# Modulation rows in one go ahead of the indexer's scores, logits inside the recurrence's last pass, and matmul moving operands at the weights' remainder by 256 bytes

## What is computed

```python
mod = jnp.dot(silu(c), w_ada) + b_ada            # 6 x 1024 values
sh1, sc1, ga1, sh2, sc2, ga2 = split(mod, 6)
xn = rms_norm(h, g_mix) * (1.0 + sc1) + sh1
q, k, v, qi, ki, wi, xr, yr, gate_a, gate_b = split(xn @ w_in + b_in)
attn = dsa_attention(q, k, v, qi, ki, wi, rel_bias)   # 8 indexer heads score, top 128 keys
rnn = rg_lru(causal_dwconv(xr), ...) * gelu(yr)
h = h + ga1 * ((sigmoid(gate_a) * (attn @ w_o_attn) + sigmoid(gate_b) * (rnn @ w_o_rnn)) @ w_out)
xn = rms_norm(h, g_ffn) * (1.0 + sc2) + sh2
h = h + ga2 * ((silu(conv(gate)) * conv(val)) @ w_down)
# second block: [meta; h] -> w_in_2 (9 x 1024 columns) -> HGRN2 and convolution -> w_out_2,
# then w_up_2, w_down_2, final norm, meta tokens dropped
```

## Time and profile before

| | |
|---|---|
| runs | 1821.69 us median of 3, 1819.59 to 1823.01 |
| profiled execution, own time | 1822.29 us |
| its span | 1820.4 us |
| mean granted TensorE clock | 0.985 of 2.4 GHz |
| busy: PE, PE weight loads, POOL, DVE, ACT | 97%, 86%, 81%, 59%, 29% |
| matmuls | 11430, each with a weight load |

### The profile page before, as it was taken

One profiled execution on the slowest core, in us unless ns is written; L12 is line 12 of the kernel. 1 busy time (PEld: TensorE's weight loads), 2 busy tenths in 40 slices (PEclk: granted clock), 3 DMA queues, 4 the chain that ended last, 5 costly groups with the idle time before them and its releaser, 6 DMA issues.

```text
span 1820.4 us, 33550 instructions
## 1 busy us (share of the span) xinstructions
PE 1766.3 (97%) x11430; PEld 1565.1 (86%) x11430; DVE 1068.6 (59%) x1677; ACT 526.4 (29%) x775; POOL 1476.2 (81%) x2245
## 2 busy tenths in 40 slices
PE   4889999999999999999899999999999999999997
PEld 2667776677899999888799999999999999999886
DVE  6887987845566777522656655665665455555102
ACT  3235664330221111100443443443343211111001
POOL 1869996559899999999678877876886999989885
PEclk8899999999999999999999999999999999999999
DMA  9644232222222222333222222222221322222332
GB/s 365 237 155 137 87 100 83 103 94 93 91 90 90 90 91 91 101 103 98 67 71 81 82 70 71 82 70 70 82 82 59 102 94 92 92 92 92 104 104 93
DMA packets 55328, 184.42 MB, mean 101 GB/s; under 512 B 6673, under 2 KB 9905, under 8 KB 55250
## 3 DMA queue, kind: packets, MB, share of 16 engines
q1 hardware_dynamic: 52018, 177.53, 29.7%
q10 hardware_dynamic: 3232, 5.77, 0.9%
HBM read 178.56 MB, written 4.72 MB: 101 GB/s over the span
## 4 chain that ended last, share of the span: by engine, by line
PE 91%; DVE 3%; POOL 2%; DMA 2%; ACT 1%; issue 1%; SPq 1%; ACTq 0%; DVEq 0%; POOLq 0%
PE gp L400 28%; PE gp L401 28%; PE gp L402 27%; PE A L727 2%; POOL Wlo L391 1%; DMA AW<-ada 1%; PE A L526 1%; DMA raw<-units 1%; PE A L496 1%; PE A L559 1%; PE gp L585 1%; PE A L774 0%; PE A L577 0%; PE A L723 0%; SPq L328 0%
## 5 line engine op out<-in xcount | busy, mean ns | idle before, releaser
L391 POOL TENSOR_TENSOR Wlo<-raw,Whi 128x256 fp32r<-128x256 f32 x1120 | 974.9, 891 | 46.8
L400 PE MATMUL gp<-XNhi,Whi 128*128 128x264 f32 (+3 forms) x2736 | 848.6, 310 | 26.9 <-POOL Wlo L391 18.3
L401 PE MATMUL gp<-XNlo,Whi 128*128 128x264 f32 (+3 forms) x2736 | 837.0, 306 | 0.0
L402 PE MATMUL gp<-XNhi,Wlo 128*128 128x264 f32 (+3 forms) x2736 | 834.2, 305 | 0.0
L400 PEld LDWEIGHTS gp<-XNhi,Whi 128*128 128x128 f32 x2736 | 517.9, 189 | 65.9 <-POOL Wlo L391 19.8
L401 PEld LDWEIGHTS gp<-XNlo,Whi 128*128 128x128 f32 x2736 | 518.1, 189 | 24.4 <-issue 2.2
L402 PEld LDWEIGHTS gp<-XNhi,Wlo 128*128 128x128 f32 x2736 | 517.1, 189 | 23.4
L387 POOL TENSOR_TENSOR probe<-raw 1x1 f32<-1x1 f32 x560 | 181.1, 323 | 278.3 <-PE gp L402 211.5
L388 POOL TENSOR_SCALAR Whi<-raw 128x512 fp32r<-128x512 f32 x560 | 346.0, 618 | 0.0
L400 PE MATMUL gp<-AChi,Whi 128*128 128x512 f32 (+1 forms) x374 | 142.8, 382 | 0.0
L402 PE MATMUL gp<-AChi,Wlo 128*128 128x512 f32 (+1 forms) x374 | 142.6, 381 | 0.0
(11 more groups left out here) (314 smaller groups left out, 2270.5 us busy)
## 6 DMA issues: line engine op xcount, KB each, us to landing
raw<-units SPq DMA_DIRECT2D x280, 512.0 KB, 3.5
AW<-ada SPq DMA_DIRECT2D x40, 512.0 KB, 7.1
AWL<-ada SPq DMA_DIRECT2D x8, 512.0 KB, 3.6
bias_rows<-RB ACTq DMA_DIRECT2D x1, 2560.0 KB, 20.9
H<-xT SPq DMA_DIRECT2D x1, 2048.0 KB, 8.3
BIAS<-bias_rows ACTq DMA_DIRECT2D x1, 2048.0 KB, 8.9
out<-H SPq DMA_DIRECT2D x8, 256.0 KB, 2.2
WG<-gatew ACTq DMA_DIRECT2D x8, 128.0 KB, 2.0
```

Source lines behind the costliest of these rows:

```text
L391: ins = pool.tensor_tensor(lo[:, c:c + UNIT // 4], src[:, c:c + UNIT // 4], hi[:, c:c + UNIT // 4].bitcast(F32), ALU.subtract)
L400: pe.matmul(dst, Whi[s][:, k, :], rhi, start=start, stop=False)
L401: pe.matmul(dst, Whi[s][:, k, :], rlo, start=False, stop=False)
L402: return pe.matmul(dst, Wlo[s][:, k, :], rhi, start=False, stop=stop)
```

## The change

It has three parts, and one smaller one for the wait at the norm.

**Addresses and spans.** `XNhi`, `XNlo`, `M2hi` and `M2lo` get rows of 576 words (2304 bytes, nine times 256). A tile `fill` of 56 words moves what lies behind it. Norms write `XN` at `x0` = 0 for both 512-word and 514-word uses in the first block, at 2 or 0 in the second block's, and at 16 only for the mixer, where the 528-word product starts at 0. Spans become 256 + 272 and 256 + 258. The built program then has `Whi0` at 63104, `XNhi` at 18048, `XNlo` at 36480, `AChi` at 117888, `MGhi` at 183424, `RNhi` at 134272, `M2hi` at 117888, `M2lo` at 136320, all with remainder 128. So d is 0 for every product of units, but for the second half of each pair in the second `up`, which starts 2 words on (d = 8).

**DVE's order.** All 24 rows in one go ahead of the scores, the small chain behind the scores and ahead of block 0's convolution, and `logits(0, 0, 1)` between the last scan and its product.

**Norm.** Nine plain fp32 matmuls of 256 words into an unused part of `gp1` after `stats(2)`; the wait for `con_in` moves ahead of them.

```diff
+ROW = 576
-AHEAD = [0, 4, 2, 2, 3, 3, 3, 3, 2, 2]
+AHEAD = [0, 4, 4, 4, 3, 4, 3, 2]
 def spans(n):
-    return [(0, n)] if n <= 512 else [(0, (n // 2 + 1) // 2 * 2), ...]
+    return [(0, n)] if n <= 512 else [(0, HALF), (HALF, n - HALF)]
...
-        XNhi = sb("XNhi", [P, KC, T], F32R)
-        XNlo = sb("XNlo", [P, KC, T], F32R)
+        XNhi = sb("XNhi", [P, KC, ROW], F32R)
+        XNlo = sb("XNlo", [P, KC, ROW], F32R)
...
+        sb("fill", [P, 56])
...
-            M2hi = sb("M2hi", [P, KC, T], F32R, f)
+            M2hi = sb("M2hi", [P, KC, ROW], F32R, f)
...
-        NORMS = [dict(c0=META, n=S, feeds=0, h0=None), dict(c0=META, n=S, feeds=1, h0=0),
-                 dict(c0=META, n=S, feeds=2, h0=KC), dict(c0=META - 2, n=S + 2, feeds=3, h0=2 * KC),
+        NORMS = [dict(c0=META, x0=0, n=S, feeds=0, h0=None), dict(c0=META, x0=2, n=S, feeds=1, h0=0),
+                 dict(c0=META, x0=META, n=S, feeds=2, h0=KC), dict(c0=META - 2, x0=0, n=S + 2, feeds=3, h0=2 * KC),
...
                     load_mid(ADA_FIRST + c)
-            sp.dma_start(CON[:, C_ONE:], consts[:, C_ONE:]).then_inc(con_in, 16)
+                if u == len(AHEAD) - 1:
+                    sp.dma_start(CON[:, C_ONE:], consts[:, C_ONE:]).then_inc(con_in, 16)
...
             stats(2)
-
+            pe.wait_ge(con_in, 16)
+            for _ in range(9):
+                pe.matmul(gp[1][:, 1024 - HALF:1024], ident, CON[:, 0:HALF], start=True, stop=True)
             pe.wait_ge(meta_xn, 1)
-            pe.wait_ge(con_in, 16)
...
-            up(U_UP2, G_UP2, 3, ((S + 2, META - 2), (S, META)), 3)
+            up(U_UP2, G_UP2, 3, ((S + 2, 0), (S, 2)), 3)
...
-            act.wait_ge(lam_done, 1)
             act.wait_ge(score_acc, NH * (QT - 1))
...
                 act.wait_ge(rnn_done, b + 1)
+                if b == 0:
+                    act.wait_ge(lam_done, 1)
...
+            act.preload_act_table(ACT.Exp)
             early_gate(0)
             exps(0, 0)
...
-            modulation(ADA_FIRST, ADA_FIRST + 16)
-            dve.wait_ge(lb_exp, 2)
...
-            dve.drain().then_inc(lam_done, 1)
...
+            modulation(ADA_FIRST, ADA_MID)
             dve.wait_ge(con_in, 16)
             dve.wait_ge(wi_mm, 1)
...
-                if n in (11, 17):
-                    c = ADA_FIRST + 16 + (0 if n == 11 else 2)
-                    modulation(c, c + 2)
...
             dve.memset(XR[:, 0:3], 0.0).then_inc(xr_pad, 1)
+            dve.wait_ge(lb_exp, 2)
...
+            dve.drain().then_inc(lam_done, 1)
...
-                if b == 0:
-                    modulation(ADA_MID - 4, ADA_MID)
...
                     dve.tensor_tensor_scan(HS[:, :], DA[:, :], UU[:, :], 0.0, ALU.mult, ALU.add)
                     dve.drain()
+                    if b == KC:
+                        logits(0, 0, 1)
                     dve.wait_ge(gelu_ready, b)
...
-            logits(0, 0, 1)
+            dve.drain()
+            logits(0, 1, 0)
             for i in range(1, QT):
                 dve.tensor_scalar(NEG[i][:, :], SC[i][:, :], TAKEN, MASKED, ALU.not_equal, ALU.mult)
             dve.drain()
-            logits(0, 1, 0)
             probabilities(0, 0)
```

More of the change, by code:

```diff
@@ L498, in score @@
                           start=True, stop=True).then_inc(score_mm, 1)
-            first_pair(0, 0, 0, ((S, META), (S, META)))
+            first_pair(0, 0, 0, ((S, 0), (S, 0)))
             for u in range(2, U_RNN):
                 pe.wait_ge(gp_free[u % 2], slot_free(u))
-                unit(u, u % 2, gp[u % 2], S, XNhi, XNlo, META, range(KC), last=KC - 1).then_inc(unit_done, 1)
+                unit(u, u % 2, gp[u % 2], S, XNhi, XNlo, 0, range(KC), last=KC - 1).then_inc(unit_done, 1)
                 if u == U_WI + 1:
@@ L532, in _ @@
                     pe.wait_ge(gp_free[g % 2], slot_free(G_RNN, g))
-                    unit(U_RNN + g, g % 2, gp[g % 2], S, XNhi, XNlo, META, range(KC), last=KC - 1).then_inc(unit_done, 1)
+                    unit(U_RNN + g, g % 2, gp[g % 2], S, XNhi, XNlo, 0, range(KC), last=KC - 1).then_inc(unit_done, 1)
                     if b and c == 0:
@@ L539, in _ @@
                 pe.wait_ge(gp_free[c], slot_free(G_KV))
-                unit(u, u % 2, gp[c], S, XNhi, XNlo, META, range(KC), last=KC - 1).then_inc(unit_done, 1)
+                unit(u, u % 2, gp[c], S, XNhi, XNlo, 0, range(KC), last=KC - 1).then_inc(unit_done, 1)
                 if c == 0:
@@ L600, in early_gate @@
                     pe.wait_ge(gp_free[c], slot_free(G_GA, c))
-                mm = unit(U_GA + c, c, gp[c], S, XNhi, XNlo, META, range(4 * b, 4 * b + 4), first=4 * b, last=KC - 1)
+                mm = unit(U_GA + c, c, gp[c], S, XNhi, XNlo, 0, range(4 * b, 4 * b + 4), first=4 * b, last=KC - 1)
                 if b:
@@ new lines, in probabilities @@
+            def probabilities(i, r):
+                dve.wait_ge(exp_done, NH * i + 4 * (r + 1))
+                dve.reciprocal(rr[:, r, :], rs[:, r, :])
+                dve.drain()
+                for s in range(4):
+                    pr = PR[:, r, s, 0:(i + 1) * P]
+                    dve.tensor_scalar(pr, pr, rr[:, r, s:s + 1], None, ALU.mult)
+                dve.drain().then_inc(p_ready, 1)
+            dve.wait_ge(bias_saved, 16)
+            dve.memset(XR[:, 0:3], 0.0).then_inc(xr_pad, 1)
@@ L1487, in _ @@
             shift = MOD[:, 3 * KC:4 * KC].rearrange("p (k o) -> p k o", o=1)
-            for c in (META - 2, META - 1):
+            for c in range(2):
                 dve.tensor_copy(XNhi[:, :, c:c + 1], shift)
```

120 lines of the change are left out of this document (55 added, 65 removed).

## The result

| | before | after |
|---|---|---|
| median of 20 runs | 1821.3 us | 1823.38 us |
| lowest, highest | 1817.94, 1823.76 | 1821.32, 1824.97 |
| profiled execution, own time and span | 1822.29, 1820.4 | 1823.94, 1822.2 |
| mean granted clock | 0.985 | 0.989 |

The ratio is 1.0013, with a 95% interval of 1.0007 to 1.0018: 2.4 us longer by the ratio, within the 0.2% that count as no change. The forecast was 1806.6 us with a range of 1787 to 1822, so the time lies outside. It stands beside the first rival's figure (1823.3 us, the distance does nothing), but not by its mechanism: the addresses did more than forecast, a gain in the rows of 512 words and a loss in the rows cut in two.

A forecast was written before the change was run, and what follows sets the result against it. PE, busy 60.00 of 60 us in the first up and down stages, was taken as the bound, besides its pauses. 1822.3 - 16.7 + 6.3 - 3.5 - 1.2 = 1807.2, less 0.6 for the median: 1806.6 us, range 1787 to 1822.

The forecast's parts named there:

- first rival: Whole kernel: the distance between operand addresses does nothing, time 1823.3 us; chance 0.13.
- Part 1: Addresses: matching moving rows to the weights shortens matmul steps throughout, gain 16.7 us, lower bound nothing.
- AC, MG, RN, AT at 512 words: Products on these tiles: 1470 matmuls step 230.2 ns instead of 233.3, gain 4.6 us.
- XN at 512 words: 512-word XN products without the second up stage: 1056 matmuls, 232.3 to 230.3 ns, gain 2.1 us.
- second up stage, 512-word halves at 8: Second up stage's 528 matmuls at distance 8, which no row has: taken as no change.
- mixer, rows cut in two: Mixer: 3456 matmuls step 119.3 ns instead of 120.9, gain 5.5 us.
- first up stage and M2: First up stage and second output product: 2496 matmuls, 119.15 to 117.5 ns, gain 4.1 us.
- second up stage, 514 words: Second up stage: 1056 matmuls, at 117.9 ns already, gain 0.4 us.
- POOL's ceiling: Up stage: POOL, busy 57.71 of 60 us, lets PE gain only its lead, about 4 us; term left whole.
- Part 2: DVE's order at the start: scores gain 2.8 us, but PE stops 6 us at gates(0); loss 6.3 us.
- Part 3: End of the recurrence: logits directly follow the scan, shorter pause and no clock fall; gain 3.5 us.
- Part 4: Second block's norm: nine matmuls fill the pause and keep the clock up, blocks wait for XNlo; gain 1.2 us.

The follow-up runs named there:

- E4: The kernel before with the change's addresses, pitch, fill and spans but the old order: 1823.83 us, ratio 1.0012.
- E1: Whole computation left out, PE alone runs 56 short streams of matmul blocks at varied distance and cut: 228.02 and 228.53 ns for one setting run twice.
- E6: The changed kernel with distance 0 only for 512-word rows, old pitch and spans in both up stages and mixer, M2 at distance 8: 1810.01 us, ratio 0.9947.
- E3: The changed order with the addresses and spans of the kernel before: 1820.17 us, ratio 0.9996.
- E11: E7 with both up stages at pitch 576 and distance 8, spans 258/256: 1809.37 us, ratio 0.9930.
- E12: The kernel before with one unused tile of 56 words ahead of the frames, nothing else changed: 1811.75 us, ratio 0.9943.
- E2: The streams of E1 with POOL splitting weight units all the while: every one of 56 means the same within 0.01 ns.
- E8: Whole computation left out, PE alone runs ten long streams of 20 units: 121.14, 226.79 and 233.44 ns a matmul in three of them.
- E7: E6 with the small chain moved behind the first convolution: 1808.72 us, ratio 0.9939.
- E9: E7 with half of the small chain moved on behind the third convolution: 1814.10 us, ratio 0.9957.

## Why the prediction was wrong

**Part 1 failed, on its sign for two-span rows.** Of the 16.7 us forecast as a gain none came: the addresses as a whole cost 2.2 (E4).

| term | forecast | measured |
|---|---|---|
| AC, MG, RN, AT at 512 words | -4.6 | AC -3.5 and -2.6, MG -1.3, RN -0.4 in the after column, AT -0.6: -8.4 |
| XN at 512 words | -2.1 | step 232.3 to 227.9 ns; the stage -0.65 (E4), and some -0.5 beside AT between RN and MG |
| second up stage, 512-word halves at 8 | 0 | 231.9 to 233.5 ns, +0.85 |
| mixer, rows cut in two | -5.5 | +4.0 (E4) |
| first up stage and M2 | -4.1 | +4.1 and +0.7 |
| second up stage, 514 words | -0.4 | +2.8 |

The step that failed is the one from single blocks to a stream: "Mixer, 3456 matmuls, 120.9 to 119.3" and "119.15 to 117.5". Both took the blocks at distance 0 out of a stage in which the distance changes with every k, and filled a stage with them. Lined up against the other distances, the kernel before spoke against it already. In its mixer the spans at d = 0 average 119.1 and 119.2 ns, but those at d = 96 have 119.0 and those at 128 119.4 to 119.5; and in its first up stage the 256-word spans at d = 64 have 116.2 against 117.5 to 117.6 at d = 0. So for rows in two spans d = 0 was one low place among others. Besides, a block's steps carry its neighbours' as well: the single matched block of the recurrence steps 226, 236 and 228 ns, one in a matched stream 227 three times. In a stream of equals, 256/258 at distance 0 stands at 121.1 to 121.6, above all but one of the two-span rows of 514 words in E1. The same step erred the other way at 512 words: matched blocks showed 230.3, a stream of them 226.8. The text had a warning in hand: the two up stages with the same addresses and different steps. It was used as a bound for the size ("can cost or give 1%"), not for the sign ("Lower bound nothing").

Also unseen: `spans` changes the cut, and the forecast took 256/272 for 264/264 as free ("the columns stay 528 in sum"). E1 has 256/272 at 122.76 ns for the change and 264/264 at 121.43 for the layout before, which over 3456 matmuls are 4.6 us for the 4.0 measured; on the way, 264/264 at distance 0 stands at 122.22, but the shares of cut and distance depend on which goes first, since they act together.

XN's gain at 512 words reached the stage only in part: 912 matmuls at 4.4 ns less are 4.0 us (means of the steps under 0.3 us). In E6 the stage is 2.4 us shorter than in E3, in E4 only 0.65 shorter than before. In E6 the first unit of each block from 4 to 7 has a step of 0.31 to 0.34 us near its start where E3 has 0.23 to 0.24, and in E4 the profile puts 1.8 us in 3 waits down to the gelu bank, none before. So a part of the gain goes into waits.

**POOL's ceiling** was a warning that held. It didn't bind in the changed kernel, where PE was slower:

```profile
POOL probe L390 <- PE gp L405: 9.4, 21, 0.5
```

is POOL's wait for PE there, 1.8 before. In E11, where PE was faster, it bound.

**Part 2** was right in its mechanism and too large. The rows end at 98.0 us (forecast near 100), the second batch of scores runs without a wait at 102.0, DVE comes free at 134.5. Then

```profile
134.47 0.60 DVE L1357 TENSOR_TENSOR LAM<-LAM 128x8 f32<-128x8 f32 x1
...
151.72 3.05 DVE L1406 SCALAR_TENSOR_TENSOR rnn_xc<-XR,V,rnn_xc 128x512 f32<-128x512 f32 x3
```

the chain takes 17.2 us, where 19.5 were put, and the convolution 3.05 for 3.40. The stop is 3.06 us instead of 6, and gates(0) come at 155.03, not 157.8. The rest is of the size forecast: half clock behind it, and a first fall near 80 us behind PE's waits for POOL, which was kept as a bound. In E3 the last gates come 2.7 us later behind the first projection than before; 6.3 were forecast.

**Part 3**: from the last gates to RN's first matmul 28.88 us before, 26.59 in E3: 2.3 us for 3.5. **Part 4**: the mixer 0.6 us shorter in E3 for 1.2 forecast, the gap ahead of it unchanged at 8.96; the nine matmuls keep the clock, and the waits for `XNlo` stay.

Parts 2 to 4 sum to +1.6 in the forecast and to -0.2 in E3's stages (-0.7 us by its ratio). What carried the error was part 1, by 19 us; that the gain at 512 words and the loss in two-span rows nearly cancel, and so land beside "does nothing", is chance.

## What to carry over

Before pricing an address layout by blocks picked from a mixed stage, run the stream itself: PE alone, the same spans, pitch and start. Here such streams gave the stages' matmul counts to one in 500, except in the first up stage, which stood 1% above its stream in both layouts with spans of 258/256 (11440 for 11307 ns, and 11307 for 11200 in E11). Give each row length its own place: 512-word rows at the weights' remainder by 256 bytes, two-span rows where a stream says, and look for the tile that is off by a few words first (E12). And when PE gets faster, read the lead of the engine that feeds it: in E11 it was used up in some 170 us, the stage kept 0.7 us of its gain, and the next one, begun without a lead, gave back 1.4.

## Not expected of the hardware

- The step of a 512-word fp32r matmul is 226.8 ns when both moving operands start at the weights' remainder by 256 bytes and 233.4 when 32 bytes off; with only the lo rows off it is 234.2, with only the hi rows 232.3 (E1, in short streams where the matched rows have 228.0).
- At 256 words it is the other way: two equal spans of 256 words step 120.5 ns at distance 0 and 117.3 at 32 (E1). The 256-word matmuls of the second down stage show it in the kernel: 116.7 ns before, 119.8 after, over 130 steps.
- POOL at work changes none of the streams' means by more than 0.01 ns (E2), while a lone change of span order at distance 0 makes 1.1 ns.
- One pitch, start and cut has two steady patterns: 11440 ns for two units in the kernel's stage and 11307 in a stream (E8), 11307 and 11200 at distance 8 (E11, E8). Open.
- A wait of 3.06 us at the gates was followed by a clock of 0.57, one of 2.8 us in E7 by none below 1, and 0.84 was granted over the 22 us that hold one of 7.1 us in E9.
